# Sample states, last pooling rows and y rows off TensorE, in the one-core layer of an HGRN2 and pooling decoder

## The reference, cut to what matters

```
proj = rmsnorm(x) @ w_in                 # q | f | v | g | u, 5 x 1024 columns
S_new = diag(f) S + k^T v                # per head; for a sample token: 128x128 state S from memory
o     = q S_new                          # prompt: the same recurrence, chunk by chunk
pool  = trailing means of u over 2/4/8/16 tokens, minus u
h = x + concat(rmsnorm(o) * silu(g), pool @ w_pool) @ w_out
h = h + swiglu(rmsnorm(h)) @ w_down
h = h + sigmoid(h @ w_ple_gate) * rmsnorm(p @ w_ple)
y = rmsnorm(h) ; also out: all states S_new, the last 15 rows of u
```

## Time and profile before

| what | value |
|---|---|
| median of 3 runs | 1169.81 us (1169.33 to 1170.16) |
| the profiled execution's own time | 1170.06 us |
| its span | 1168.2 us |
| PE busy | 1156.9 us, 99% of the span, 12469 matmuls |
| DVE busy | 1006.4 us, 86% |
| ACT busy | 565.1 us, 48% |
| TensorE clock granted | 1.00 (2.4 GHz) in every slice but the last one |
| memory traffic | 201 GB/s over the span |

### The profile page before, as it was taken

One profiled execution on the slowest core, in us unless ns is written; L12 is line 12 of the kernel. 1 busy time (PEld: TensorE's weight loads), 2 busy tenths in 40 slices (PEclk: granted clock), 3 DMA queues, 4 the chain that ended last, 5 costly groups with the idle time before them and its releaser, 6 DMA issues.

```text
span 1168.2 us, 31003 instructions
## 1 busy us (share of the span) xinstructions
PE 1156.9 (99%) x12469; PEld 1037.3 (89%) x12469; DVE 1006.4 (86%) x1575; ACT 565.1 (48%) x810; POOL 55.5 (5%) x80
## 2 busy tenths in 40 slices
PE   8999999999999999999999999999999999999997
PEld 7888888888888899899998999989989999999886
DVE  6778799778867898998989989888899999998687
ACT  6545645654546644444444444444444444444443
POOL 2122310100000200000000000000000000000000
PEclk9999999999999999999999999999999999999999
DMA  8767876766566566666666666666666666667561
GB/s 253 238 200 207 237 217 192 232 190 190 181 211 199 180 216 199 195 194 204 215 200 195 194 202 215 203 193 194 201 199 215 202 199 207 206 199 242 163 190 75
DMA packets 193385, 234.92 MB, mean 201 GB/s; under 512 B 8010, under 2 KB 153777, under 8 KB 193040
## 3 DMA queue, kind: packets, MB, share of 16 engines
q1 hardware_dynamic: 187984, 221.08, 60.4%
q0 software_dynamic: 3968, 11.89, 3.6%
q10 hardware_dynamic: 1360, 0.92, 0.3%
HBM read 226.89 MB, written 7.43 MB: 201 GB/s over the span
## 4 chain that ended last, share of the span: by engine, by line
PE 93%; DVE 4%; ACT 1%; issue 1%; DMA 0%; DVEq 0%; ACTq 0%
PE acc L2322 13%; PE acc L1924 10%; PE acc L1926 10%; PE acc L1928 10%; PE acc L2363 7%; PE acc L2325 6%; PE acc L2324 6%; PE acc L2303 6%; PE acc L2305 6%; PE wrk L2303 4%; PE wrk L2305 4%; PE acc L2365 2%; PE acc L2366 2%; DVE hl L977 2%; PE wrk L2081 1%
## 5 line engine op out<-in xcount | busy, mean ns | idle before, releaser
L977 DVE SCALAR_TENSOR_TENSOR hl<-raw,hl 128x1024 f16<-128x1024 f32 x414 | 493.7, 1220 | 51.7 <-ACT hl L610 49.0
L610 ACT ACTIVATE hl<-raw 128x1024 f16<-128x1024 f32 x414 | 420.3, 1051 | 168.8 <-DMA raw<-in_w_down_dram 88.0
L2322 PE MATMUL acc<-nrm,hl 128*128 128x264 f16 x1344 | 274.8, 276 | 0.3 <-DVE tg L1481 0.3
L1926 PE MATMUL acc<-nrm,hl 128*128 128x264 f16 x920 | 253.9, 276 | 0.0
L1928 PE MATMUL acc<-nrm,hl 128*128 128x264 f16 x920 | 253.9, 276 | 0.0
L1924 PE MATMUL acc<-nrm,hl 128*128 128x264 f16 x920 | 253.9, 276 | 0.0
L2324 PE MATMUL acc<-nrm,hl 128*128 128x264 f16 x672 | 185.5, 276 | 0.0
L2325 PE MATMUL acc<-nrm,hl 128*128 128x264 f16 x672 | 185.5, 276 | 0.0
L2322 PEld LDWEIGHTS acc<-nrm,hl 128*128 128x128 f16 x1344 | 129.0, 98 | 18.1 <-DVE tg L1481 0.6
L2363 PE MATMUL acc<-big,hl 128*128 128x264 f16 x704 | 130.2, 276 | 0.0
L1924 PEld LDWEIGHTS acc<-nrm,hl 128*128 128x128 f16 x920 | 90.2, 98 | 13.2 <-issue 0.3
(11 more groups left out here) (492 smaller groups left out, 2241.9 us busy)
## 6 DMA issues: line engine op xcount, KB each, us to landing
raw<-in_w_gate_up_dram SPq DMA_DIRECT2D x168, 512.0 KB, 4.6
raw<-in_w_down_dram SPq DMA_DIRECT2D x88, 512.0 KB, 4.0
raw<-in_w_in_dram SPq DMA_DIRECT2D x80, 512.0 KB, 4.7
raw<-in_w_out_dram SPq DMA_DIRECT2D x32, 512.0 KB, 5.0
raw<-in_w_ple_gate_dram SPq DMA_DIRECT2D x32, 512.0 KB, 5.0
state<-in_state_hgrn_dram POOLq DMA_DIRECT2D x8, 512.0 KB, 6.6
out_new_hgrn_sample_dram<-state POOLq DMA_DIRECT2D x8, 512.0 KB, 5.3
raw<-in_w_gate_up_dram SPq DMA_DIRECT2D x16, 256.0 KB, 3.8
```

Of the source, the lines that this page charges most:

```text
L610: nc.scalar.activation(hi[:, st.hl_slot(j, half), :], raw[:, st.raw_slot(j), :], ACT.Copy, scale=WSCALE).then_inc(hi_done, 1)
L977: stt(lo[:, st.hl_slot(j, half), :], raw[:, st.raw_slot(j), :], WSCALE, hi[:, st.hl_slot(j, half), :], ALU.mult, ALU.subtract).then_inc(lo ...
L1926: mm(out, wh, x_lo[:, kt, :], start=False, stop=False)
L2322: mm(out, wh, n_hi[:, kt, :], start=jj == 0 and kk == 0, stop=False, skip_group_check=bool(up))
```

## The change

- **Sample states.** The `kv` transposes, `outer` and `pair_states` go. PE transposes the v of the samples once for four heads (`vs`, two jobs in all). ACT copies the 32x128 rows and writes them to memory (`v_rows`), waits for that one block later, and issues two loads that spread a head's eight v rows over all 128 partitions (`v_bc`, 512 KB each). ACT scales each 128x128 state by f and each 128x128 block of `v_bc` by k (`sample_part`, r = 0 to 3: eight activations of 128x128 at each r, 128 in all). DVE adds the two, one 128x1024 tensor_tensor for a head (`new_states`).
- **Last pooling rows.** DVE turns 32x32 blocks of u (`nc.vector.transpose`), POOL stores them with eight DMAs of 128-byte pieces.
- **y rows.** DVE turns 32x32 blocks of h (`turned`), four DMAs write 512 features in pieces of 128 bytes to memory (`y_rows`), eight read them back as rows (`y_turns`; 0 and 1 on POOL, 2 on SP behind its last weight load).
- **Squares of the end** go from DVE to ACT (`squares`), the sums stay on DVE (`gate_sum`). Loops over two groups are written out.
- **Places.** The pairs start at 27, 38, 51 and 60, the sample sums move two blocks back, the third and fourth pooling sum from 81 and 84 to 83 and 85.

```diff
-SAMPLE_AT = (26, 38, 50, 58)
-BUF_AT, U_LAST_AT, OSS_AT = 44, (73, 81), 71
-RMS_AT, ROOT_AT, SAMPLE_ROOT_AT = 64, 65, 72
-O_NORM_AT, O_MIX_AT, SAMPLE_MIX_AT = (66, 67, 69, 71), (68, 70, 72, 74), 75
-WINDOW_AT = (75, 77, 81, 84)
+SAMPLE_AT = (27, 38, 51, 60)
+ROWS_AT = (25, 49)
+BUF_AT, U_LAST_AT, OSS_AT = 44, (73, 81), 73
+RMS_AT, ROOT_AT, SAMPLE_ROOT_AT = 64, 65, 74
+O_NORM_AT, O_MIX_AT, SAMPLE_MIX_AT = (66, 67, 69, 71), (68, 70, 72, 74), 76
+WINDOW_AT = (75, 77, 83, 85)
...
+        def y_turns(queue, c):
+
+            queue.wait_ge(y_turned, 2 * (c + 1))
+            for q in range(4):
+                dst = y_rows[c].rearrange("r m (k q f) -> q r (m k) f", q=4, f=32)[q]
+                src = y_blk[32 * q:32 * q + 32, c].rearrange("r m k f -> r (m k) f")
+                queue.dma_start(dst, src).then_inc(y_out[c], 16)
+            queue.wait_ge(y_out[c], 16 * 4)
+            for a in range(2):
+                for m in range(4):
+                    queue.dma_start(y_tok[32 * m:32 * m + 32, a, y_cols(c)], y_rows[c, :, 4 * a + m, :]).then_inc(y_in[c], 16)
...
+            def value_rows(c, r):
+
+                if r == 0:
+                    wait_job(f"vs_{c}")
+                    nc.scalar.activation(vs_tok, wrk[0:4 * NSAMP, JOB[f"vs_{c}"] % JOB_BANKS, 0:P], ACT.Copy)\
+                        .then_inc(drained["act"], 1)
+                    act.wait_ge(drained["act"], drain_of(f"vs_{c}")[1])
+                    act.dma_start(v_rows[c], vs_tok).then_inc(vs_out, 16)
+                elif r == 1:
+                    act.wait_ge(vs_out, 16 * (c + 1))
+                    for h in range(2):
+                        rows_to_all(4 * c + h)
...
             def sample_part(p, r):
 
-                if r == 0:
-                    wait_job(f"kv_{p}")
-                    if p:
-                        wait_job(f"ou_{p - 1}_3")
-                    nc.scalar.activation(kv_smp, wrk[:, JOB[f"kv_{p}"] % JOB_BANKS, :].bitcast(F16)
...
+                if r in range(4):
+                    h, old = 2 * p + r % 2, r // 2 == p % 2
+                    x, gains = (state[:, h % 2], f_all) if old else (v_bc[h % 2], k_all)
+                    if old:
+                        act.wait_ge(state_in[h % 2], 16 * (p + 1))
+                        act.wait_ge(acc_free, TPG * (3 * (p // 2) + 3))
+                    else:
+                        act.wait_ge(v_bc_in[h % 2], 16 * (p + 1))
+                    for b in range(NSAMP):
+                        last = nc.scalar.activation(x[:, b, :], x[:, b, :], ACT.Copy, scale=gains[:, h, SEQ + b:SEQ + b + 1])
+                    last.then_inc(state_kept if old else kv_ready, 1)
                 elif r in (5, 6):
                     h = 2 * p + r - 5
-                    act.wait_ge(drained["dve"], drain_of(f"ou_{p}_3")[1])
+                    act.wait_ge(state_new, h + 1)
...
+                    if p % 2 == 0:
+                        rows_to_all(h + 2)
...
+            def squares(i, ns=range(TPG)):
+
+                for n in ns:
+                    act.wait_ge(gate_chain, i * TPG + n + 1)
+                    if i or n >= 2:
+                        act.wait_ge(gate_sum_done, i * TPG + n - 1)
+                    nc.scalar.activation((h_sq, h_sq1)[n % 2], h_all[:, i * TPG + n, :], ACT.Square).then_inc(gate_sq, 1)
...
-            def pair_states(p, bs):
...
+            def new_states(h):
+
+                dve.wait_ge(state_kept, h + 1)
+                dve.wait_ge(kv_ready, h + 1)
+                tt(state[:, h % 2], state[:, h % 2], v_bc[h % 2], ALU.add).then_inc(state_new, 1)
...
-                if r in (2, 4):
-                    pair_states(p, (r - 2, r - 1))
+                if r in (3, 4):
+                    new_states(2 * p + r - 3)
...
+            def turned(c):
+
+                for n in range(2):
+                    dve.wait_ge(hg_ready, c * TPG + (2 * n + 2))
+                    of = h_all[:, c * TPG + 2 * n:c * TPG + 2 * n + 2, 0:SEQ].rearrange("p k (m f) -> p k m f", f=32)
+                    to = y_blk[:, c, :, 2 * n:2 * n + 2, :].rearrange("p m k f -> p k m f")
+                    nc.vector.transpose(to, of).then_inc(y_turned, 1)
...
-            dve.wait_ge(drained["act"], drain_of("yp_2_1")[1])
+            for c in range(len(Y_GROUPS)):
+                dve.wait_ge(y_in[c], 16 * 8)
             scaled(1, slice(0, Y_EARLY))
...
-            def sample_kv(p):
...
-            def outer(p, bs):
...
-            def last_u(n):
...
-            def y_transposes(c):
```

More of the change, by code:

```diff
@@ L199 @@
             JOBS += [(f"sf_{_c}", "act")]
+    if _b in ROWS_AT:
+        JOBS += [(f"vs_{ROWS_AT.index(_b)}", "act")]
     for _p in range(PAIRS):
         _r = _b - SAMPLE_AT[_p]
[L202 to L206, removed]
+        if _r == 10:
             JOBS += [(f"os_{_p}", "dve")]
@@ L553, in _ @@
             pool.wait_ge(drained["dve"], drain_of(f"n1_{KT - 1}")[1])
[L554 to L558, removed]
+            nc.gpsimd.memset(scores[:, 0:2], 0.0).then_inc(zero_ready, 1)
             pool.wait_ge(masks_ready, 1)
@@ L599, in _ @@
                 nc.gpsimd.tensor_tensor(n_lo[:, k, :], ntmp(k), n_hi[:, k, :], ALU.subtract).then_inc(n_odd, 1)
+            for c in range(len(Y_GROUPS) - 1):
+                y_turns(pool, c)
         @block.scalar
@@ L812, in _ @@
                     sample_part(p, b - SAMPLE_AT[p])
[L813 to L818, removed]
+                for c in range(QUADS):
+                    value_rows(c, b - ROWS_AT[c])
                 if b == PD_HI_AT:
@@ L915, in _ @@
             act.wait_ge(e_ready, KT)
[L916 to L918 removed]
+            def squares(i, ns=range(TPG)):
[4 more added lines that the diff above has]
+                    nc.scalar.activation((h_sq, h_sq1)[n % 2], h_all[:, i * TPG + n, :], ACT.Square).then_inc(gate_sq, 1)
+            group(S_GATE, 0, lambda: (gates(S_GATE, 0, range(TPG), C_H), squares(0)), between=lambda: next_high(S_DOWN.groups - 1))
+            for i in range(1, S_GATE.groups - 1):
+                group(S_GATE, i, lambda: (gates(S_GATE, i, range(TPG), C_H, reuse=True), squares(i)))
             last = S_GATE.groups - 1
[L921 to L924 removed]
             def late_sigmoid(n, cols, value):
@@ L930, in late_sigmoid @@
                 nc.scalar.activation(gate_t[:, n, cols], src, ACT.Sigmoid, scale=C_H).then_inc(tail_sig, 1)
-            split(S_GATE, last, 4)
-            split(S_GATE, last, 5)
-            y_taken(0)
+            for j in range(4, 7):
+                split(S_GATE, last, j)
             gates(S_GATE, last, (0,), C_H, reuse=True)
-            split(S_GATE, last, 6)
             split(S_GATE, last, 7)
-            y_taken(1)
+            squares(last, (0,))
             gates(S_GATE, last, (1,), C_H, reuse=True)
-            y_taken(2)
+            squares(last, (1,))
             late_sigmoid(2, LATE_COLS, 1)
@@ L2045, in prompt_v @@
                     yield
-            def outer(p, bs):
-                if bs[0] == 0:
-                    pe.wait_ge(drained["act"], drain_of(f"kv_{p}")[1])
-                for bb in bs:
-                    out = job(f"ou_{p}_{bb}")
-                    rows = slice(32 * bb, 32 * bb + 4)
-                    for n in range(4):
-                        last = mm(out[:, n * P:(n + 1) * P], kv_smp[rows, 0, n // 2, n % 2, :],
-                                  kv_smp[rows, 1, n // 2, n % 2, :], start=True, stop=True)
-                    last.then_inc(job_done, 1)
             def diagonal(c):
@@ L2183, in buffer_sums @@
                     if k == 7:
-                        last.then_inc(job_done, 1)
-                    yield
-            def last_u(n):
-                pe.wait_ge(acc_free, (9 + n) * TPG)
-                out = job(f"ut_{n}")
-                for k in range(4):
-                    last = nc.tensor.transpose(out[0:POOL_BUF + NSAMP, k * P:(k + 1) * P],
-                                               u_all[:, 4 * n + k, SEQ - POOL_BUF:TOK], ident[:])
-                    if k == 3:
                         last.then_inc(job_done, 1)
@@ L2390, in _ @@
             down_group(S_DOWN.groups - 1, 1, final=True)
-            def y_transposes(c):
-                ks = Y_GROUPS[c]
-                pe.wait_ge(hg_ready, ks[-1] + 1)
-                for a in range(2):
-                    out = job(f"yp_{c}_{a}")
-                    for n, k in enumerate(ks):
-                        last = nc.tensor.transpose(out[:, n * P:(n + 1) * P], h_all[:, k, a * P:(a + 1) * P], ident[:])
-                        if k == ks[-1]:
-                            last.then_inc(job_done, 1)
-                        yield
             stream(S_GATE, 0, n_hi, n_lo, ready=lambda j: pe.wait_ge(n_ready, KT // 2 + 2 * j + 2))
```

158 lines of the change are left out of this document (75 added, 83 removed).

## The result

| | median us | runs | ratio to before |
|---|---|---|---|
| before | 1169.95 | 1169.33 to 1170.16 (4) | |
| after | 1178.32 | 1177.81 to 1180.10 (4) | 1.0070, 95% interval 1.0058 to 1.0082 |

The kernel is 8.4 us slower. 1176.3 was forecast, with slower as the likeliest sign.

A forecast was written before the change was run, and what follows sets the result against it. PE's own work was taken to set the time (busy 99%). Removed work -7.8 and pooling move -0.8 plus stalls 15.1 gave +6.5 us, so 1176.3 us; own range 1171.5 to 1181, with rivals 1163 to 1182.

The forecast's parts named there:

- The deciding price: ACT's small state-scaling activations: 0.29 us each, 2.3 us a visit of eight; below 0.235 us the faster rival would hold.
- Rival 1: PE's work decides: activations 0.20 us apart, visits 1.6 us, about 1163 us, or 1166 with some stalls; chance 0.31.
- What PE loses: Work leaving PE: outer 2.7, kv 1.8, last pooling rows 0.9, y rows 2.6, less 0.2 added; -7.8 us, nothing hiding it.
- Pair 0: Blocks 27 to 30: ACT reaches the eviction of block 31 late, PE stalls 2.1 us.
- Now from 103.4: Blocks 27 to 30: from ACT's end of keys at 103.4, visits, splits, v copy and keys run to 116.6.
- Pair 1: Blocks 38 to 41: f tile eviction costs PE 0.5 us, late key packs stall score jobs 2.4 us in sum.
- Pair 2: Blocks 51 to 54: ACT reaches block 55's eviction near 205.5, PE stalls 3.5 us; write wait taken as 3 us from issue.
- Pair 3: Blocks 60 to 63: ACT work 9.6 us; stalls 1.8 at block 64, 1.4 at o transposes, 1.6 at block 72.
- Pooling sums: Between evictions at 83 and 87, DVE's splits and sums take 11.5 us against PE's 10.8: stall 1.3, 0.8 removed.
- The end: Last gate group and y rows: 0.2 us lost at late tiles, 0.3 on y rows landing about 13 us after turning.
- Rival 3: Last y rows land 4 us late because 128-byte pieces move at half rate; alone 1166, with forecast 1180 us; chance 0.12.
- rival 4: Spread v_bc loads of blocks 51 to 54 take 10 us, not 5, stopping ACT and DVE: +2 us; chance 0.1.

The follow-up runs named there:

- Experiment 4: Kernel after with four instead of eight activations a visit, half the samples unscaled (states wrong, for time alone): 1166.77 us, ratio 0.9971.
- experiment 1: Kernel before with only the change's y rows, and the squares on ACT: 1167.40 us, ratio 0.9973.
- experiment 9: Kernel before with the change's y part and last pooling rows, sample states and pooling sums as before: 1169.17 us, ratio 0.9992.
- experiment 12: Kernel of experiment 9 with second u transpose, sample sums and third pooling sum at block 80 instead of 81: 1167.45 us, ratio 0.9977.
- experiment 3: Kernel after with the third and fourth pooling sums back at blocks 81 and 84: 1178.44 us, ratio 1.0068.
- experiment 8: Kernel after with DVE packing the sample values at the head of blocks 24 and 48, not at the end: 1181.60 us, ratio 1.0098.
- experiment 2: Kernel after without the y rows and squares part; sample states, last pooling rows and later sums stay: 1182.36 us, ratio 1.0096.
- experiment 10: Kernel after with the same sixteen visits of eight activations spread over other blocks: 1175.20 us, ratio 1.0035.
- experiment 11: Kernel of experiment 10 with DVE packing the sample values at the head of blocks 24 and 48: 1172.40 us, ratio 1.0021.
- experiment 5: Kernel after with ACT scaling only v_bc; DVE multiplies the old state and adds, one instruction a sample: 1174.75 us, ratio 1.0045.
- experiment 6: Kernel after with POOL scaling v_bc, one product a head, and ACT only the old states: 1173.30 us, ratio 1.0024.
- experiment 7: Kernel after without ACT visits: POOL scales v_bc, DVE multiplies and adds in one instruction a sample: 1173.09 us, ratio 1.0025.

## Why the prediction was right, point by point

- **The deciding price** held: 0.29 us an activation, 2.33 us a visit. Rival 1 needed less than 0.235. Experiment 4 shows what that price decides: with half the work in a visit (about 1.2 us) the kernel takes 1166.8 us, nearly what rival 1 forecast for visits of 1.6 us (1163 to 1166).
- **What PE loses**, -7.8: the y rows' -2.6 shows as -3.2 +- 1.3 in experiment 1. The term of the last pooling rows, -0.9 with "nothing hides this work", was wrong by itself: work ahead of an eviction for which PE waits gives nothing (experiment 9: not faster but 2.2 us slower than the y part alone, of which the traces explain 0.7; experiment 12: no faster).
- **Pair 0**: 2.1 forecast, 3.3 measured. The step "Now from 103.4" failed. It took the keys of block 27 to end as before, but ACT's wait for the write of the v rows and its two loads (0.84 us) stand ahead of that block's split and keys; the prediction counted both in pair 2 and not here. The keys end at 106.31, 2.9 us late. Of these, 1.65 are the late start of this execution (last section), which PE shares, and the other 1.2 are what the stall exceeds the forecast by. In experiment 3, without the late start, the keys end at 104.24, 0.8 late, and the stall is 3.0. From the end of the keys on, the sum held: 13.3 us to the eviction against 13.2 worked out.
- **Pair 1**: 0.5 and 2.4 forecast, 0.7 and 2.6 measured.
- **Pair 2**: 3.5 forecast at block 56, 2.0 measured. Missing was the place ahead of it: "added are two transposes, 0.2" costed the jobs and not their wait for DVE's copy, 0.35 and 1.95 us. Experiment 8 shows that these are one account: without the one, block 56 waits 3.4, about the forecast 3.5. The write of the v rows was taken as 3 us from issue; the loads behind it went out 1.95 us after its issue in pair 2, but 5.2 us after it in pair 0.
- **Pair 3**: 1.8, 1.4 and 1.6 forecast, 1.3, 2.3 and 0.7 measured; sum 4.8 against 4.3. The prediction's "9.6" is not the sum of its parts: they make 8.55, and it is with 8.55 and not with 9.6 that the stall of 1.8 at block 64 comes out.
- **Pooling sums**: 1.3 forecast at block 88, 1.7 measured, against 0.8 regained. With the pooling rows this part of the change gives nothing.
- **The end**: 0.5 forecast, nothing measured. The blocks were turned at 1155.8 and the rows landed at 1167.26: 11.5 us in place of 13. Two errors met: issuing took longer than forecast (2.85 us for four DMAs and 4.34 for eight, against 1.5 and 3), and landing took less (3.0 and 2.1 us on SP, against 4.6 and 3). The forecast's own parts make 12.1 us and not 13, and its lateness of 1.1 us less the 1 that is hidden makes 0.1 and not 0.3. Rival 3 (rows 4 us late) didn't come. Neither did rival 4: ACT had no wait for a spread load.
- **Sum**: stalls 15.1 forecast, 16.9 measured; with -8.6 this gives +8.3 us, and the medians differ by 8.4. The two profiled executions differ by 10.0 us, which is 8.3 and the 1.65 of the late start. That forecast and result agree so well is partly luck: pair 0 was 1.2 us too low, pair 2 1.5 too high, and the waits for packed values, 2.3 us, were missing.

The clock is not the cause of the 8.4 us: the mean granted clock of the four executions after is 0.9973, that of 68 timed executions of the kernel before 0.9979, which is 0.7 us as an estimate. Still open is where in the kernel the other executions lose time to the clock, since only one of each version has a profile.

## What to carry to other kernels

Work that is taken from the engine that sets the time pays only up to the next place where that engine would wait for another. Before moving work to an engine that is half idle, follow its order through the blocks in which it lands, and the engine behind it too: here ACT's idle time lay elsewhere, and DVE, which goes in step behind ACT's splits, passed each delay on to PE. When a wait is removed, ask which one was just behind it; if the answer is a fixed order on a full engine, the wait only moves.

## What was not expected of the hardware

**Long waits can cost clock as well.** In the kernel before the granted clock is full outside the last slice. In experiment 3 (columns: stretch, us, PE busy with matmuls, granted clock, DMA share, GB/s):

```profile
116.00:120.00 4.00, 1.34 (x10) 0.94 0.64 185
120.00:124.00 4.00, 4.00 (x25) 0.64 0.47 133
124.00:128.00 4.00, 4.00 (x38) 1.00 0.78 248
248.00:252.00 4.00, 1.94 (x18) 1.00 0.97 274
252.00:256.00 4.00, 3.89 (x20) 0.58 0.75 252
```

PE had waited 2.8 us until 118.7 and ran at full clock for 0.8 us; then for some 3 us its matmuls started 0.22 us apart and not 0.11 (the lower level, 1.2 of 2.4 GHz): 25 in a stretch in place of 38, 1.4 us lost beside the wait itself. The same stands behind its wait of 2.2 us at 250, behind two such waits in each of experiments 2 and 8, and behind one in 10 (2.0 us) and in 11 (2.5 us). It doesn't follow each time: the waits of 3.15 and 2.16 us in the kernel after had no such stretch. There the clock was low from 16 us on, at the start of the projection:

```profile
16.00:20.00 4.00, 3.38 (x16) 0.58 0.56 147
20.00:24.00 4.00, 4.00 (x38) 1.00 0.80 248
```

Its first eviction came 1.65 us later than before, and that goes a long way towards the 1.8 us by which the profiled execution lies above its median. The late start is not of the change's making: five other profiles (experiments 1, 5, 6, 10 and 11) show a low stretch between 10 and 20 us, in code that is the same in all kernels here. Nor does it always cost as much: in experiment 1 block 84 is asked for only 0.26 us later than in the kernel before. The Trainium skill, TensorE: Matmul & The Clock Gate, Part 1, names the same two levels and puts the choice down to PE's recent activity. The traces show the two levels (0.5 and 1.00 of full clock) and, in experiments 2, 3, 8, 10 and 11, the lower one behind a wait; why the same wait has it in one execution and not in another, no run here shows. The prediction's sum had no term for it.

**A GpSimd product holds up VectorE's products**, 4.26 us for 1.41 (experiment 7), while ACT's visits beside it kept to 2.34 us (experiment 6).
